# The first stage's large transfers on one queue, and its four modulation jobs each closed before the next, with filler matmuls between them

## What is computed

```python
sh, sc, gt = jnp.split(jax.nn.silu(c) @ w_ada[l] + b_ada[l], 3, axis=-1)
sh_c, sc_c, gt_c = jnp.split(jax.nn.silu(c_ctx) @ w_ada[l] + b_ada[l], 3, axis=-1)
h = rms_norm(x, norm_g[l]) * (1 + sc[:, None]) + sh[:, None]
hc = rms_norm(ctx, norm_g[l]) * (1 + sc_c) + sh_c
... = split_proj(h @ w_in[l])
```

## Time and profile before

| | us |
|---|---|
| median of 3 runs | 3651.17 (3649.71 to 3651.17) |
| span of the profiled execution | 3652.5 |
| its first stage, to the second stage's first matmul | 59.1 |
| PE busy in the span | 3533.3 (97%) |

### The profile page before, as it was taken

How to read it: one execution, slowest core, us unless ns; L and a number is a source line. 1 busy time by engine, 2 the same in 40 slices (tenths; PEclk the granted TensorE clock), 3 DMA queues, 4 the chain that set the end, 5 groups by cost and what they waited for, 6 DMA issues and landing times. The chain is left out here.

```text
span 3652.5 us, 53885 instructions
## 1 busy us (share of the span) xinstructions
PE 3533.3 (97%) x20756; PEld 2540.0 (70%) x20756; DVE 2282.5 (62%) x4223; ACT 1269.1 (35%) x2394; POOL 1044.2 (29%) x981
## 2 busy tenths in 40 slices
PE   7999998999999999989999999999998999999999
PEld 4656556789754655567897468555655588888888
DVE  4277454765675377557656661675548777894488
ACT  3255434632632255446426221674232311001100
POOL 2400064666541400256665330002224200000000
PEclk9999999999999999999999999999999999999999
DMA  5101142001112101110011221000000377552254
GB/s 199 49 18 42 59 153 93 2 8 52 37 61 92 50 18 41 61 36 1 1 47 49 88 74 58 3 22 24 24 24 19 113 273 264 184 179 98 92 184 161
DMA packets 142267, 279.01 MB, mean 76 GB/s; under 512 B 5728, under 2 KB 50784, under 8 KB 139584
## 3 DMA queue, kind: packets, MB, share of 16 engines
q1 hardware_dynamic: 114848, 221.89, 17.5%
q10 hardware_dynamic: 25872, 47.71, 3.7%
q0 software_dynamic: 1296, 5.97, 0.4%
HBM read 231.52 MB, written 44.04 MB: 75 GB/s over the span
## 5 line engine op out<-in xcount | busy, mean ns | idle before, releaser
L1003 PE MATMUL ps<-ring,hT 128*128 128x512 f32 (+3 forms) x1296 | 375.8, 446 | 9.6 <-DVE nrm_b L1184 4.4
L1003 PEld LDWEIGHTS ps<-ring,hT 128*128 128x128 f32 x1296 | 217.9, 191 | 145.9 <-issue 122.9
L1544 DVE TENSOR_REDUCE stat_a<-ps 128x1 f32<-128x1280 f32 (+1 forms) x144 | 190.7, 1365 | 153.9 <-PE ps L1388 153.9
L1442 PE MATMUL ps<-hT,ring 128*128 128x512 f32 (+1 forms) x640 | 280.2, 551 | 0.0
L1753 POOL TENSOR_TENSOR P_b<-P_b,stat_b 128x1280 f32<-128x1280 f32 (+1 forms) x108 | 227.8, 2130 | 174.6 <-DVE stat_b L1769 135.6
L2842 ACT ACTIVATE hid<-hid 128x1024 f32<-128x1024 f32 x32 | 33.8, 1057 | 482.5 <-DVE hid L2889 427.7
L1484 ACT ACTIVATE YT<-ps,stat_a 128x1280 f32<-128x1280 f32 (+1 forms) x144 | 176.5, 1231 | 25.4 <-DVE stat_a L1544 25.4
L2669 PE MATMUL ps<-Y 128*128 128x256 f32 x768 | 171.1, 379 | 0.9 <-DVE Y L2654 0.5
L1528 POOL COPY rb_a<-stat_a 128x64 f32<-128x64 f32 x72 | 14.6, 236 | 538.8 <-DVE YT L1557 538.8
L2669 PEld LDWEIGHTS ps<-Y 128*128 128x128 f32 x768 | 145.8, 190 | 21.3 <-issue 1.5
L1413 PEld LDWEIGHTS ps<-const,YT 128*128 128x128 f32 x656 | 71.6, 142 | 97.3 <-issue 86.5
(11 more groups left out here) (612 smaller groups left out, 8141.8 us busy)
## 6 DMA issues: line engine op xcount, KB each, us to landing
ring<-in_w_up SPq DMA_DIRECT2D x16, 2048.0 KB, 9.1
ring<-down_sums SPq DMA_DIRECT2D x16, 2048.0 KB, 8.3
ring<-in_w_in SPq DMA_DIRECT2D x14, 2048.0 KB, 8.1
ring<-in_w_down SPq DMA_DIRECT2D x12, 2048.0 KB, 7.9
adaw_b<-in_w_ada SPq DMA_DIRECT2D x16, 1024.0 KB, 5.2
ring<-in_w_out SPq DMA_DIRECT2D x6, 2048.0 KB, 7.9
Wd<-in_w_down ACTq DMA_DIRECT2D x11, 1024.0 KB, 7.3
down_sums<-Wd ACTq DMA_DIRECT2D x11, 1024.0 KB, 7.2
```

The lines of the kernel that those rows point to most:

```text
L1003: mm = pe.matmul(ps[:, bank(n), 0:hi - lo], hT[:, k, t * P:(t + 1) * P], w[:, k, lo:hi], start=(k == 0), stop=(k == KC - 1))
L1442: mm = pe.matmul(ps[:, GB, 0:hi - lo], pr.view(i0 + c)[:, k, b % 4 * P:(b % 4 + 1) * P], hT[:, k, lo:hi], start=(k == 0), stop=(k == KC - 1))
L1544: dve.tensor_reduce(st[:, i % 4, m:m + 1], scored_at(i, m), AX, ALU.max, negate=True)\
```

## The change

All large transfers go to SP's queue in this order: four parameter transfers, ten token tiles, four modulation blocks, ring slot 0, the tables, ring slot 1. SP no longer waits for the blocks ahead of the ring; at its end it waits for the tables. POOL keeps the identity alone, ACT issues nothing. The jobs take the blocks in the order 0, 1, 2, 3. On PE `columns(j - 1)` moves ahead of `rows(j)`, and between them stand 14 matmuls of `keep_busy`, three times in all. The transposes stay ahead of all jobs.

```diff
-    ORDER = (0, 2, 3, 1)
...
-            for i in range(0, NT, 2):
+            for i in range(NT):
                 sp.dma_start(big[:, i, :], x_rows(i)).then_inc(*S[f"x_in_{i}"].inc(16))
-            for n in range(2):
+            for n in range(JOBS):
                 sp.dma_start(adaw[:, n], ada_src(n)).then_inc(*S[f"ada_in_{n}"].inc(16))
-            for n in range(JOBS):
-                sp.wait_ge(*S[f"ada_in_{n}"](16))
-            for i in range(SLOTS):
+            pr.load(sp, 0)
+            sp.dma_start(t["const"][:, SOON:N1], const_src[:, SOON:N1]).then_inc(*S["tables_in"].inc(16))
+            for i in range(1, SLOTS):
                 pr.load(sp, i)
+            sp.wait_ge(*S["tables_in"](16))
...
             pool.dma_start(t["const"][:, 0:SOON], const_src[:, 0:SOON]).then_inc(*S["const_in"].inc(16))
-            for i in range(1, NT, 2):
-                pool.dma_start(big[:, i, :], x_rows(i)).then_inc(*S[f"x_odd_in_{i}"].inc(16))
-            for n in range(JOBS):
-                pool.wait_ge(*S[f"ada_in_{n}"](16))
-            pool.dma_start(t["const"][:, SOON:N1], const_src[:, SOON:N1]).then_inc(*S["const_in"].inc(16))
-            pool.wait_ge(*S["const_in"](32))
...
-                act.wait_ge(*S[f"x_odd_in_{i}" if i % 2 else f"x_in_{i}"](16))
+                act.wait_ge(*S[f"x_in_{i}"](16))
...
-            for n in range(2, JOBS):
-                act.dma_start(adaw[:, n], ada_src(n)).then_inc(*S[f"ada_in_{n}"].inc(16))
             root(0)
...
-                modulation_rows(pe, ps[:, 4 + j % 2, :], cs, adaw[:, ORDER[j]]).then_inc(*S["rows_done"].inc())
+                modulation_rows(pe, ps[:, 4 + j % 2, :], cs, adaw[:, j]).then_inc(*S["rows_done"].inc())
...
             for j in range(JOBS):
-                rows(j)
                 if j:
                     columns(j - 1)
+                    keep_busy(pr, pe, 7, ident, 14)
+                rows(j)
             columns(JOBS - 1)
             keep_busy(pr, pe, 7, ident, 10)
             pr.arrived(pe, 0)
```

More of the change, by code:

```diff
@@ L404, in rows @@
             def rows(j):
-                pe.wait_ge(*S[f"ada_in_{ORDER[j]}"](16))
+                pe.wait_ge(*S[f"ada_in_{j}"](16))
                 if j >= 2:
                     pe.wait_ge(*S["rows_kept"](j - 1))
-                modulation_rows(pe, ps[:, 4 + j % 2, :], cs, adaw[:, ORDER[j]]).then_inc(*S["rows_done"].inc())
+                modulation_rows(pe, ps[:, 4 + j % 2, :], cs, adaw[:, j]).then_inc(*S["rows_done"].inc())
             def columns(j):
@@ L412, in columns @@
                 for m in range(4):
-                    mm = pe.matmul(cols[:, 4 * ORDER[j] + m, :], row[:, j % 2, m * P:(m + 1) * P], t["rows"], start=True, stop=True)
+                    mm = pe.matmul(cols[:, 4 * j + m, :], row[:, j % 2, m * P:(m + 1) * P], t["rows"], start=True, stop=True)
                 mm.then_inc(*S["cols_done"].inc())
```

## The result

The changed kernel takes 3662.11 us (median of 9 runs, 3656.43 to 3666.54) against 3651.17 us: the ratio is 1.0031, with a 95% interval of 1.0022 to 1.0041. It is slower by about 11 us; the forecast was 3663.2, in a range of 3658 to 3667.

What follows compares the result with a forecast made beforehand. PE's own order of work was taken to bound the first stage from 37.39 us on, with no slack behind it. Jobs and fillers +13.8 and earlier start -1.8 gave +12.0 us: 3651.2 to 3663.2, range 3658 to 3667.

Steps and rivals of the forecast that it cites:

- No transfer of weights ends a wait on the path before: First stage: no modulation or projection weight transfer ends a wait in the kernel before; moving them there: gain and cost 0.
- The earlier start, -1.8 us: Ahead of the jobs: tiles on one queue and ACT without transfer issues bring root(0) and the first job 1.8 us earlier.
- the best case: ACT's five squares run without a wait from 8.44 us, gaining 1.1 us; root(0) at about 14.6 at best.
- the slow start of SP's queue: SP's first token tile half a microsecond later cuts the squares' gain to 0.7 us; a worse start could take it all.
- The job, 3.77 us: PE's rows, DVE's copy, handover and columns run one after another: 3.77 us per job, 15.1 us for four.
- The handover from DVE's copy to PE: Between DVE's copy and PE's columns in each job: 0.1 us, allowed 0.05 to 0.3.
- The filler, 3.25 us each: On PE between jobs: 14 matmuls take 3.25 us, three times 9.75 us, paid in full.
- Sum: First stage: jobs and fillers 24.85 us instead of 11.05, so +13.8; earlier start -1.8; net +12.0 us.
- The free filler: Rival 1: PE fits the filler into waits at no cost; +2.3 us, 3653.5 us; chance 5%.
- the low clock among the jobs: Rival 3: the granted clock falls during the jobs' new waits; +10.8 us more, 3674 us; chance 4%.
- the slow queue: Rival 4: one queue is slower than several; at 250 GB/s the stage is 3.8 us longer, 3667 us; chance 3%.
- jobs could run as the blocks land: Rival 2: only the last block counts, -4.4 us, 3646.8 us; rows(0) must start by 23.6 to break even; chance 2%.

Runs made afterwards that it cites:

- the earlier trace: The profiled execution of the kernel before, nothing changed; its span was 3652.5 us, against a median of 3651.17 us.
- the filler in the wait: Changed kernel with each filler of 14 matmuls moved ahead of columns, between rows and the wait for DVE's copy; 3659.52 us, ratio 1.0029 to the kernel before.

## Why the prediction held, step by step

*No transfer of weights ends a wait on the path before.* Held: with the jobs overlapped and the transfers moved, the gain is 2.9 us, all of it through an earlier start. The landings came a little later than forecast (blocks at 24.6, 30.0, 35.5 and 42.1 us against 24, 29.5, 35 and 40.3, slot 0 at 47.4 against 46), still some ten microseconds or more ahead of their readers.

*The earlier start, -1.8 us.* It was -2.94 between the two traces. What the change itself brings was sized about right. Root(0) came at 14.40 and not at 14.75:

```profile
14.40 0.21 ACT L221 ACTIVATE rs<-ssq 128x5 f32<-128x5 f32 x1 [0.30 <-DVE ssq L360]
```

That is 2.15 us before the 16.55 of the earlier trace rows, and 1.73 before the 16.13 of the second trace of the kernel before. ACT's squares ran back to back from 8.25 to 14.1, as the best case said, and the slow start of SP's queue that was allowed for did not come. The other 0.8 us is the second group of transposes, 6.55 us long (27.90 to 34.45) instead of 7.35, with the clock at 0.50, by the windows, for some 3.4 us instead of 6.8. This part is chance: with the filler in the wait, the program up to there being the same, the clock was low for 6.8 us again, the group took 7.41, and the first job came at 35.35, near the 35.6 of the forecast. The prediction had it as an end of the range (0.9), and that end was too short: in the run without fillers the group took 5.65 us. It was read off the first group (6.71), but that one, too, went slowly in part: in the kernel before, PE did 12 matmuls from 20 to 22 us, as many as at 0.50 in the earlier trace rows, although the windows view gives that stretch as 1.00.

*The job, 3.77 us.* Measured without filler: 3.72. The handover from DVE's copy to PE, which no row showed, was taken as 0.1 and bounded by 0.05 and 0.3. In the changed kernel DVE's copy ended at 36.45 + 0.69 = 37.14, and PE's columns started at 37.19: 0.05 us.

```profile
36.45 0.69 DVE L348 COPY row<-ps 128x512 f32<-128x512 f32 x1 [1.63 <-PE ps L263]
```

*The filler, 3.25 us each.* Measured 3.30 from start to start, and 9.70 for the three together when they were taken away (24.52 - 14.82), where the sum has 9.75. That they are paid in full was shown by taking them away and by moving them.

*Sum.* +13.5 for jobs and fillers (13.8 forecast) and -2.9 for the start (-1.8) make +10.5 for the stage, and the medians differ by 10.9. The forecast was +12.0; of its error of 1.5 us, 1.1 lies in the term of the start and 0.3 in the jobs. The sign and the size of the loss rest on the jobs and fillers, which the two traces that have them in this order give alike (24.52 and 24.51 us); that the median came within 1.1 us of the forecast is in part luck, since the first job's start varies by 1.7 us between traces and the median of the kernel before by 1.3 between sets of runs.

*The profiled execution against the median.* The front of this document compared the span of the profiled execution with the median. The runs after show that the time of a run is 1.75 us longer than its span (3660.65 and 3658.9). So the profiled execution of the kernel before was an estimated 3.1 us above the median and not 1.3. The sum was not harmed, because it was made from differences inside the first stage; taken from the two spans, the result would have looked like 6.4 us.

*The rivals.* The free filler, the low clock among the jobs and the slow queue are each refuted by a run or a row above. That jobs could run as the blocks land was out of reach: the first job starts at 33.7 at the earliest in any run, and 23.6 was needed.

## What to carry to other kernels

Filler matmuls that keep PE busy were free only where it stood idle, and as PE works in program order it must meet them in front of the wait that they are to cover: the same 14 matmuls cost 3.2 us each time between two jobs, 2.2 in front of a wait of 0.8, and nothing in an idle gap of 4.4. Before work is spread out to follow transfers as they land, compare the landing times with the moment at which the engine gets there; here the blocks had landed ten to thirteen microseconds before. A move of a transfer that is worth nothing by itself can be what lets another gain through (here by the estimate for ring slot 0), so look at what would be late next for every microsecond that is to be won.

## What the runs showed of the hardware

In or just behind the idle gap between the two groups of transposes the granted clock fell to 0.50 in some executions and not in others, and came back after different times. Of the eight traces without a filler in the gap it fell in seven, for some 3.4 us in four of them and 6.8 in three. Idle for 3.89 us, it stayed at 1.00 in the run without fillers (first row); with the filler in the wait, idle for 4.60 us and the same program up to there, the mean over the second group was 0.63.

```profile
28.00:34.00 6.00, 5.48 (x44) 4.46 (x48) 5.76 (x9) 2.59 (x5) 0.00 (x0) 1.00 1.05 387
```

```profile
28.00:36.00 8.00, 8.00 (x48) 7.47 (x52) 6.00 (x9) 2.94 (x5) 0.00 (x0) 0.63 1.04 386
```

The second group then takes 5.65 us (28.05 to 33.70) in the one, 7.41 in the other (27.94 to 35.35): 1.8 us that belong to no edit. Since the runs of one kernel spread over some 10 us and the faster ones have the higher mean clock, the same chance in other stages is the likely source of that spread; a difference of 2 to 3 us in such a kernel is seen in the stage, over several traces, and not in the time.

One queue alone carried the stage's transfers at the rate that several had: 383 to 388 GB/s from 28 to 32 us in the changed kernel, 386 and 387 in the earlier trace rows. SP was held in its issues meanwhile, up to 7.5 us for one block (line 289 above), at no cost here: what followed on SP, the ring slots and the tables, had no reader yet; slot 0 was issued at 26.7 and landed at 47.4, and its reader came at 62.06.
